# Uneven column pieces in three of the four key/value projection tiles of a decoder step

## The chip, the cores and the metric

The kernel runs on one core of one Trainium2 chip. The metric is device time in microseconds (us) of one execution; lower is better. TensorE is called PE here, its weight loads PEld, VectorE DVE, ScalarE ACT, GpSimd POOL and SyncE SP.

## What is computed

One inference step of a two-layer decoder over 1024 prompt tokens and 64 sample tokens (8 sequences of 8), 1088 token columns in all, with a model width of 2048. Layer 0 is a gated convolution mixer, layer 1 a sliding-window attention that reads one shared key/value projection. The part that matters here is that projection:

```python
kv = rms_norm(h, kv_norm) @ w_kv          # (tokens, 2048) @ (2048, 512)
k, v = jnp.split(kv, 2, axis=-1)          # 4 key/value heads of 64 each
```

Its inputs and outputs are float32. The result is needed for the attention of layer 1 and for the key and value caches that the step returns.

## The kernel before

All projections are made by one routine, `tile(n, z)` of the TensorE program (from line 499). A tile is one block of 128 output features for all 1088 token columns; there are 132 of them, each with 2048 input features in 16 steps `k` of 128. The activations lie in SBUF as `u_hi[128, 16, 1088]` and `u_lo[128, 16, 1088]`, and the weights of a tile as `w_hi` and `w_lo` in four quarters of 4 steps each: every float32 value is split into a rounded part (type float32r) and a rest. A product is the sum of three: hi by hi (line 512), hi weights by the rest of the activations (line 513), and the rest of the weights by hi (line 515).

One PSUM accumulator `z` has three banks of 512 float32 columns, `z[128, 3, 512]`. A matrix product writes one bank, so the 1088 columns go in three pieces, set by the table `CHUNKS`: columns 0 to 363, 364 to 727 and 728 to 1087. A step `k` thus issues nine matrix products: line 512 and line 513 for the first piece, the same for the second and the third, and then line 515 for the three pieces. Each product has a weight load of its own (128 rows by 128 columns) ahead of it in the trace. A tile makes 16 x 9 = 144 products.

```python
for c in cs:
    o = z[:, c, 0:CHUNKS[c][1]]
    pe.matmul(o, w_hi[:, q, at:at + P], chunk(u_hi[:, k, :], c), start=(i == 0), stop=False)
    pe.matmul(o, w_hi[:, q, at:at + P], chunk(u_lo[:, k, :], c), start=False, stop=False)
for c in cs:
    mm = pe.matmul(z[:, c, 0:CHUNKS[c][1]], w_lo[:, q, at:at + P], chunk(u_hi[:, k, :], c),
                   start=False, stop=(i == KT - 1))
```

The key/value projection is tiles 64 to 67 (`N_KV` is 64). Even tiles write `z_even`, odd ones `z_odd`. The two V tiles (64, 65) come first, then the two K tiles (66, 67). Their order on PE is written out by hand: tile 64, interleaved with the sums of squares of the residual stream (`sum_sq`, line 526); a wait for the root of the norm; tile 65; tile 66; then the transposes of V (lines 595 and 598), which use `aux`, and which wait for ACT's copies (lines 900 and 903); then tile 67. After that come the query and gate tiles (68 to 99), with the attention between their steps.

Three things surround a tile. SP loads its weights by quarters (`load_w`). For tiles 64 to 99 POOL multiplies a quarter by the norm's gain (`gain_w`, line 1005), ACT rounds it to `w_hi` once PE has used the same quarter of the tile before (`split_w`, line 730), and POOL subtracts to get `w_lo` (`rest_w`, line 1013); PE waits for that quarter by quarter. When PE has used all four quarters, DVE reads the accumulator by the same three pieces, multiplies it by the norm factor and writes it to SBUF (`read_z`, line 1261), and a later tile may use the accumulator again. After tile 67 ACT waits for that read, issues three DMAs for K (lines 914 to 916), and only then rounds the weights of tile 68.

Of the kernel before, what the change touches and what calls it, by code (L numbers as in the profile page):

```python
# [31 lines left out]
ALU = mybir.AluOpType  # L32
# [3 lines left out]
P = 128  # L36
D = 2048
KT = D // P
# [2 lines left out]
TS = SB * SS  # L41
T = TP + TS
CHUNKS = [(0, 364), (364, 364), (728, 360)]
ALL, HEAD, TAIL = (0, 1, 2), (0, 1), (2,)
TH = CHUNKS[2][0]
TT = T - TH
# [10 lines left out]
N_GLU, N_GATE, N_OUTA, N_KV, N_QG, N_OUTB, N_OUTC, N_END = 0, 32, 48, 64, 68, 100, 116, 132  # L57
# [32 lines left out]
def trunk_kernel(nc, x_t, state_t, ck_t, cv, w, cols_in, y_t, scp_t, ckp_t, cvp, scs_t, cks_t, cvs):  # L90
    ctx = ExitStack()
    with ctx:
        def sb(name, shape, dt=F32):
            return ctx.enter_context(nc.sbuf_tensor(name, shape, dt))
# [13 lines left out]
        u_hi = sb("u_hi", [P, KT, T], F32R)  # L108
        u_lo = sb("u_lo", [P, KT, T], F32R)
        w_raw = sb("w_raw", [P, NQ, 512])  # L110
        w_hi = sb("w_hi", [P, NQ, 512], F32R)
        w_lo = sb("w_lo", [P, NQ, 512], F32R)
# [8 lines left out]
        z_odd = ctx.enter_context(nc.psum_tensor("z_odd", [P, 3, 512], F32))  # L121
        z_even = ctx.enter_context(nc.psum_tensor("z_even", [P, 3, 512], F32))
        aux = ctx.enter_context(nc.psum_tensor("aux", [P, 2, 512], F32))
        ZS = [z_even, z_odd]
        aux1 = aux[:, :, :].rearrange("p a b -> p (a b)")

        def region(at, n):
            return work[:, at:at + n]
# [12 lines left out]
        cs = cs_flat.rearrange("p (b s) -> p b s", b=SB)  # L141
# [18 lines left out]
        r_b = region(0, T)  # L160
        kvb = [region(6 * T, T), region(7 * T, T), region(8 * T, T), region(9 * T, T)]
# [116 lines left out]
        def ge(eng, s, v):  # L278

            if not (isinstance(v, int) and v <= 0):  # L280
                eng.wait_ge(s, v)

        def chunk(ap, c):
            return ap[:, CHUNKS[c][0]:CHUNKS[c][0] + CHUNKS[c][1]]

# [210 lines left out]

        @block.tensor
        def _(pe):
            def tile(n, z, before_k=None, after_k=None, order=range(KT), cs=ALL):

                ge(pe, z_read, n - 1)
                seen = [0] * NQ
                for i, k in enumerate(order):
                    if before_k is not None:
                        before_k(i)
                    q, at = k // 4, P * (k % 4)
                    if seen[q] == 0:
                        pe.wait_ge(w_lo_ready, NQ * n + q + 1)
                    seen[q] += 1
                    for c in cs:  # L510
                        o = z[:, c, 0:CHUNKS[c][1]]
                        pe.matmul(o, w_hi[:, q, at:at + P], chunk(u_hi[:, k, :], c), start=(i == 0), stop=False)  # L512
                        pe.matmul(o, w_hi[:, q, at:at + P], chunk(u_lo[:, k, :], c), start=False, stop=False)  # L513
                    for c in cs:
                        mm = pe.matmul(z[:, c, 0:CHUNKS[c][1]], w_lo[:, q, at:at + P], chunk(u_hi[:, k, :], c),  # L515
                                       start=False, stop=(i == KT - 1))
                    if seen[q] == 4:
                        mm.then_inc(w_used, 1)
                    if after_k is not None:
                        after_k(i)  # L520

            def sum_sq(i):

                pe.wait_ge(sq_ready, KT + i + 1)
                for c in range(3):
                    mm = pe.matmul(z_odd[:, c, 0:CHUNKS[c][1]], ones[:, :], chunk(sq_h[i % 2], c),
                                   start=(i == 0), stop=(i == KT - 1))
                mm.then_inc(sq_summed, 1)

            def sum_o(phase):  # L530


                first, cs, _, added = PROJ[phase]
                pe.wait_ge(o_added, added + KT - 1)
                pe.wait_ge(z_read, first + KT - 1)
                for c in cs:
                    pe.matmul(z_even[:, c, 0:CHUNKS[c][1]], ones[:, :], chunk(acc_o, c), start=True, stop=False)
                pe.wait_ge(z_read, first + KT)
                for c in cs:
                    mm = pe.matmul(z_even[:, c, 0:CHUNKS[c][1]], ones[:, :], chunk(sq_o[1], c), start=False, stop=True)  # L540
                mm.then_inc(o_summed, 1)

            pe.wait_ge(consts_ready, 6)

            pe.transpose(aux[:, 0, 0:SS], causal_ts[0:SS, :], ident[0:SS, 0:SS]).then_inc(mask_turned, 1)
            tile(0, z_even, lambda k: pe.wait_ge(u_lo_ready, k + 1))
            pe.wait_ge(sq_added, KT - 1)
            for c in range(3):
                mm = pe.matmul(z_odd[:, c, 0:CHUNKS[c][1]], ones[:, :], chunk(r_a, c), start=True, stop=True)
            mm.then_inc(sq_summed, 1)  # L550
            pe.wait_ge(var_ready, 1)
            tile(1, z_odd)
            with pe.Fori(1, KT) as i:
                tile(2 * i, z_even)
                tile(2 * i + 1, z_odd)
# [27 lines left out]

            tile(N_KV, z_even, before_h, after_h, ORDER)
            pe.wait_ge(var_ready, 4)
            tile(N_KV + 1, z_odd)
            tile(N_KV + 2, z_even)

            for t in range(2):
                pe.wait_ge(z_read, N_KV + t + 1)  # L590
                for part in range(3):
                    ge(pe, vt_read, 3 * t + (1 if part == 2 else 0))
                    if part < 2:
                        for b in range(4):
                            mm = pe.transpose(aux[:, part, P * b:P * b + P],
                                              kvb[t][:, P * (4 * part + b):P * (4 * part + b) + P], ident[:, :])
                    else:
                        mm = pe.transpose(aux[0:TS, 0, 0:P], kvb[t][:, TP:T], ident[:, :])
                    mm.then_inc(vt_ready, 1)
            tile(N_KV + 3, z_odd)  # L600

            def scores(g, jj, u):

# [398 lines left out]
        def _(pool):  # L1002
# [143 lines left out]
            def add_o(j, par, phase):  # L1146
                first, cs, _, added = PROJ[phase]
                t0, t1 = CHUNKS[cs[0]][0], sum(CHUNKS[cs[-1]])
                pool.wait_ge(z_read, first + j + 1)
                ge(pool, o_added, added + j)  # L1150
                pool.tensor_tensor(acc_o[:, t0:t1], acc_o[:, t0:t1], sq_o[par][:, t0:t1], ALU.add
                                   ).then_inc(o_added, 1)
# [86 lines left out]
        def _(dve):  # L1239
# [14 lines left out]
                t0, t1 = CHUNKS[cs[0]][0], sum(CHUNKS[cs[-1]])  # L1254
                dve.reciprocal(r[:, t0:t1], r[:, t0:t1]).then_inc(r_ready, 1)

            def read_z(n, z, out, by):

                dve.wait_ge(w_used, NQ * (n + 1))
                for c in range(3):  # L1260
                    ins = dve.tensor_tensor(chunk(out, c), z[:, c, 0:CHUNKS[c][1]], chunk(by, c), ALU.mult)  # L1261
                ins.then_inc(z_read, 1)


# [17 lines left out]
            inv_rms(r_a, z_odd, 1)  # L1282
            dve.wait_ge(r_ready, 1)
            read_z(0, z_even, sig, r_a)

            def glu(j, nxt):
# [19 lines left out]
                for i in range(2, CW):  # L1306
                    if i > 2:
                        dve.wait_ge(tap, (CW - 1) * j + i - 2)
                    acc = odd_taps if i % 2 else aux1
                    dve.scalar_tensor_tensor(out=acc, in0=cp[:, i:i + TP],  # L1310
                                             scalar=cols[:, bass.ds(C_CW + j * CW + i, 1)], in1=acc,
                                             op0=ALU.mult, op1=ALU.add).then_inc(tap, 1)
                    if i == CW // 2 and nxt:
                        read_z(2 * j + 2, z_even, sig, r_a)
# [7 lines left out]


            read_z(N_GATE, z_even, gg0[0], r_a)
            dve.wait_ge(state_out, 32 * KT)
            for c in range(3):
# [8 lines left out]
                ins = dve.tensor_tensor(var, var, sq, ALU.subtract)  # L1335
# [54 lines left out]
            for i in range(1, 4):  # L1390
                dve.wait_ge(h_out[i], 16 * KT // 4)
            for t in range(4):
                read_z(N_KV + t, ZS[t % 2], kvb[t], r_b)

            def row_max(g, jj, u):

# [188 lines left out]
```

## Time and profile before

| | us |
|---|---|
| median of 3 runs | 3379.62 |
| lowest, highest run | 3376.69, 3385.57 |
| span of the profiled execution, first to last instruction | 3378.6 |
| PE busy, PEld busy (overlapping) | 3197.5, 3077.4 |
| DVE, ACT, POOL busy | 1511.2, 854.5, 1551.1 |
| mean granted clock of TensorE | 0.974 of full speed |

The profile gives no time of its own for that execution beside its span, which is 1.0 us below the median of the runs. Times in a row of a timeline are counted from the span's start. A matrix product's recorded length reaches past the start of the next one, because products are pipelined and their ends are modelled; the distance between starts tells what one costs in a stream. A weight load's recorded length likewise reaches past the start of the product that uses it.

### The profile page before, as it was taken

Reading aid. Unit: us, or ns where it says so; the run is one execution under the profiler, and the core shown is the slowest. Engines: PE = TensorE matmul, PEld = TensorE weight load, DVE = VectorE, ACT = ScalarE, POOL = GpSimd, SP = SyncE. Lnnn points to the kernel's source line nnn. Section 1 sums busy time; section 2 is a strip of 40 time slices with the busy share of each in tenths; the row PEclk is TensorE's granted clock in tenths of the full one; section 3 lists DMA queues with packets and bytes.
Section 4 is the critical chain, followed back from the end, with each engine's and each line's share of the span. In section 5 each row is a group of like instructions: output and inputs, shape, how many; then the busy total and the mean of one; then the engine's idle time right before and its main releaser. Section 6 shows DMA issues by size and latency. Waiting matters only on the chain.

```text
span 3378.6 us, 50475 instructions
## 1 busy us (share of the span) xinstructions
PE 3197.5 (95%) x19117; PEld 3077.4 (91%) x19117; DVE 1511.2 (45%) x1745; ACT 854.5 (25%) x1708; POOL 1551.1 (46%) x1153
## 2 busy tenths in 40 slices
PE   7999999999899999999778999999999999999995
PEld 6999999999899999999668998999899899899995
DVE  6999999999711131000560433244323343500043
ACT  5121121121222132212321322222222222332232
POOL 2777877878543324333353223332233223144475
PEclk9999999999899999999899999999999999899998
DMA  4122122122132252212453112111111211333386
GB/s 158 45 64 58 46 69 58 46 69 58 57 100 87 93 171 78 73 63 70 170 190 94 36 37 63 41 37 44 47 47 41 53 38 46 118 114 87 97 295 217
DMA packets 171677, 284.87 MB, mean 84 GB/s; under 512 B 62008, under 2 KB 72504, under 8 KB 171576
## 3 DMA queue, kind: packets, MB, share of 16 engines
q1 hardware_dynamic: 127328, 222.48, 22.2%
q10 hardware_dynamic: 41912, 52.32, 4.2%
q0 software_dynamic: 2352, 8.88, 0.7%
q8 instruction: 61, 1.00, 0.1%
q14 instruction: 24, 0.20, 0.0%
HBM read 218.44 MB, written 67.15 MB: 85 GB/s over the span
## 4 chain that ended last, share of the span: by engine, by line
PE 57%; POOL 17%; issue 12%; DVE 6%; DMA 4%; ACT 2%; SPq 1%; POOLq 0%; ACTq 0%; DVEq 0%
PE z_odd L512 9%; PE z_odd L513 8%; PE z_odd L515 8%; PE z_even L512 8%; PE z_even L513 7%; PE z_even L515 7%; POOL w_lo L1013 6%; POOL work L1094 4%; PE aux L609 3%; POOL work L1086 3%; PE z_even L627 2%; DMA work<-conv_scratch 1%; PE z_even L629 1%; POOL work L1122 1%; DMA work<-out_scratch 1%
## 5 line engine op out<-in xcount | busy, mean ns | idle before, releaser
L1013 POOL TENSOR_TENSOR w_lo<-w_raw,w_hi 128x512 fp32r<-128x512 f32 x528 | 746.7, 1423 | 1452.1 <-ACT w_hi L730 1451.6
L512 PE MATMUL z_even<-u_hi,w_hi 128*128 128x364 f32 (+1 forms) x2784 | 925.1, 332 | 80.7 <-POOL u_lo L1174 33.8
L512 PE MATMUL z_odd<-u_hi,w_hi 128*128 128x364 f32 (+1 forms) x2784 | 939.0, 337 | 58.9 <-POOL w_lo L1013 58.9
L513 PE MATMUL z_odd<-u_lo,w_hi 128*128 128x364 f32 (+1 forms) x2784 | 922.5, 331 | 0.0
L513 PE MATMUL z_even<-u_lo,w_hi 128*128 128x364 f32 (+1 forms) x2784 | 921.0, 331 | 0.0
L730 ACT ACTIVATE w_hi<-w_raw 128x512 fp32r<-128x512 f32 x528 | 331.4, 630 | 1730.5 <-PE z_even L515 810.3
L515 PE MATMUL z_odd<-u_hi,w_lo 128*128 128x364 f32 (+1 forms) x2784 | 636.5, 330 | 0.0
L515 PE MATMUL z_even<-u_hi,w_lo 128*128 128x364 f32 (+1 forms) x2784 | 635.3, 329 | 0.0
L512 PEld LDWEIGHTS z_even<-u_hi,w_hi 128*128 128x128 f32 x2784 | 529.8, 190 | 99.6 <-issue 30.7
L512 PEld LDWEIGHTS z_odd<-u_hi,w_hi 128*128 128x128 f32 x2784 | 531.7, 191 | 97.3 <-POOL w_lo L1013 55.1
L513 PEld LDWEIGHTS z_odd<-u_lo,w_hi 128*128 128x128 f32 x2784 | 532.1, 191 | 0.1
L513 PEld LDWEIGHTS z_even<-u_lo,w_hi 128*128 128x128 f32 x2784 | 530.2, 190 | 0.4 <-issue 0.3
L515 PEld LDWEIGHTS z_odd<-u_hi,w_lo 128*128 128x128 f32 x2784 | 487.9, 190 | 0.0
L515 PEld LDWEIGHTS z_even<-u_hi,w_lo 128*128 128x128 f32 x2784 | 486.6, 189 | 0.0
L1310 DVE SCALAR_TENSOR_TENSOR work<-work,cols 128x1024 f32<-128x1024 f32 x224 | 419.9, 1875 | 0.0
L1310 DVE SCALAR_TENSOR_TENSOR aux<-work,cols,aux 128x1024 f32<-128x1024 f32 x240 | 306.4, 1277 | 38.2 <-ACT aux L774 38.0
L1251 DVE TENSOR_SCALAR work<-z_even 128x364 f32<-128x364 f32 (+1 forms) x6 | 2.9, 529 | 657.0 <-PE z_even L540 657.0
L1261 DVE TENSOR_TENSOR work<-z_even,work 128x364 f32<-128x364 f32 (+1 forms) x126 | 59.4, 525 | 497.5 <-PE z_even L515 497.4
L1094 POOL TENSOR_TENSOR work<-work 128x480 f32<-128x480 f32 (+3 forms) x128 | 153.6, 1200 | 10.0
L1005 POOL TENSOR_TENSOR w_raw<-w_raw,cols 128x512 f32<-128x512 f32 x144 | 148.3, 1040 | 17.5 <-DMA branch_scratch<-work 17.5
L1086 POOL TENSOR_TENSOR work<-work,cols 128x248 f32<-128x248 f32 x128 | 130.4, 1049 | 2.9 <-POOL work L1098 2.9
L609 PE MATMUL aux<-work 64*128 64x256 f32 (+1 forms) x512 | 120.8, 376 | 0.0
(148 smaller groups left out, 2405.1 us busy)
## 6 DMA issues: line engine op xcount, KB each, us to landing
w_raw<-in_w SPq DMA_DIRECT2D x528, 256.0 KB, 2.7
work<-in_x SPq DMA_DIRECT2D x32, 544.0 KB, 5.7
work<-branch_scratch SPq DMA_DIRECT2D x31, 544.0 KB, 5.5
conv_scratch<-work ACTq DMA_DIRECT2D x16, 544.0 KB, 2.7
work<-conv_scratch SPq DMA_DIRECT2D x16, 544.0 KB, 3.7
resid_scratch<-work ACTq DMA_DIRECT2D x16, 544.0 KB, 6.2
branch_scratch<-work ACTq DMA_DIRECT2D x16, 512.0 KB, 2.6
branch_scratch<-work POOLq DMA_DIRECT2D x15, 544.0 KB, 3.0
```

What stands on the lines that cost most here:

```text
L512: pe.matmul(o, w_hi[:, q, at:at + P], chunk(u_hi[:, k, :], c), start=(i == 0), stop=False)
L513: pe.matmul(o, w_hi[:, q, at:at + P], chunk(u_lo[:, k, :], c), start=False, stop=False)
L515: mm = pe.matmul(z[:, c, 0:CHUNKS[c][1]], w_lo[:, q, at:at + P], chunk(u_hi[:, k, :], c), start=False, stop=(i == KT - 1))
L609: mm = pe.matmul(s_qk[:, i, lo:2 * BLK], qf[HD * p:HD * p + HD, BLK * b:BLK * b + BLK], kd[HD * p:HD * p + HD, BLK * (b - 1) + lo:BLK * b ...
L627: mm = pe.matmul(o, vd[:, b, :], pc[:, i, :], start=True, stop=(b == 0))
L730: act.activation(w_hi[:, q, :], w_raw[:, q, :], ACT.Copy).then_inc(w_hi_ready, 1)
L1005: pool.tensor_tensor(w_raw[:, q, :].rearrange("p (k c) -> p k c", k=4), w_raw[:, q, :].rearrange("p (k c) -> p k c", k=4), cols[:, gain + ...
L1013: pool.tensor_tensor(w_lo[:, q, :], w_raw[:, q, :], w_hi[:, q, :].bitcast(F32), ALU.subtract).then_inc(w_lo_ready, 1)
L1086: ins = pool.tensor_tensor(pr[:, b], win, cols[:, bass.ds(C_CW + j * CW, CW)].unsqueeze(1).to_broadcast([P, SS, CW]), ALU.mult)
L1094: pool.tensor_tensor(pm[:, :, 0:m], pm[:, :, 0:m], pm[:, :, other:other + m], ALU.add).then_inc(pool_step, 1)
L1261: ins = dve.tensor_tensor(chunk(out, c), z[:, c, 0:CHUNKS[c][1]], chunk(by, c), ALU.mult)
L1310: dve.scalar_tensor_tensor(out=acc, in0=cp[:, i:i + TP], scalar=cols[:, bass.ds(C_CW + j * CW + i, 1)], in1=acc, op0=ALU.mult, op1=ALU.add ...
```

## The change

Tile 64 keeps the pieces 364 + 364 + 360. Tile 65 takes 512 + 512 + 64 columns, tile 66 takes 512 + 448 + 128 and tile 67 takes 512 + 320 + 256. The number of products per tile, their order, their weights and the total of columns stay as they are. DVE's reads of the three accumulators are cut at the same places.

```diff
+KV_CUTS = [CHUNKS, [(0, 512), (512, 512), (1024, 64)], [(0, 512), (512, 448), (960, 128)],
+           [(0, 512), (512, 320), (832, 256)]]
...
-            def tile(n, z, before_k=None, after_k=None, order=range(KT), cs=ALL):
+            def tile(n, z, before_k=None, after_k=None, order=range(KT), cs=ALL, cuts=CHUNKS):
...
                     for c in cs:
-                        o = z[:, c, 0:CHUNKS[c][1]]
-                        pe.matmul(o, w_hi[:, q, at:at + P], chunk(u_hi[:, k, :], c), start=(i == 0), stop=False)
-                        pe.matmul(o, w_hi[:, q, at:at + P], chunk(u_lo[:, k, :], c), start=False, stop=False)
+                        t0, m = cuts[c]
+                        pe.matmul(z[:, c, 0:m], w_hi[:, q, at:at + P], u_hi[:, k, t0:t0 + m], start=(i == 0), stop=False)
+                        pe.matmul(z[:, c, 0:m], w_hi[:, q, at:at + P], u_lo[:, k, t0:t0 + m], start=False, stop=False)
                     for c in cs:
-                        mm = pe.matmul(z[:, c, 0:CHUNKS[c][1]], w_lo[:, q, at:at + P], chunk(u_hi[:, k, :], c),
+                        t0, m = cuts[c]
+                        mm = pe.matmul(z[:, c, 0:m], w_lo[:, q, at:at + P], u_hi[:, k, t0:t0 + m],
                                        start=False, stop=(i == KT - 1))
...
-            tile(N_KV + 1, z_odd)
-            tile(N_KV + 2, z_even)
+            tile(N_KV + 1, z_odd, cuts=KV_CUTS[1])
+            tile(N_KV + 2, z_even, cuts=KV_CUTS[2])
...
-            tile(N_KV + 3, z_odd)
+            tile(N_KV + 3, z_odd, cuts=KV_CUTS[3])
...
-            def read_z(n, z, out, by):
+            def read_z(n, z, out, by, cuts=CHUNKS):
 
                 dve.wait_ge(w_used, NQ * (n + 1))
-                for c in range(3):
-                    ins = dve.tensor_tensor(chunk(out, c), z[:, c, 0:CHUNKS[c][1]], chunk(by, c), ALU.mult)
+                for c, (t0, m) in enumerate(cuts):
+                    ins = dve.tensor_tensor(out[:, t0:t0 + m], z[:, c, 0:m], by[:, t0:t0 + m], ALU.mult)
...
-                read_z(N_KV + t, ZS[t % 2], kvb[t], r_b)
+                read_z(N_KV + t, ZS[t % 2], kvb[t], r_b, KV_CUTS[t])
```

## Rows read from the trace of the kernel before

**Rows 1.** The page: span, engines' busy time, and the chain's shares by engine.
```profile
span 3378.6 us, 50475 instructions
...
PE 3197.5 (95%) x19117; PEld 3077.4 (91%) x19117; DVE 1511.2 (45%) x1745; ACT 854.5 (25%) x1708; POOL 1551.1 (46%) x1153
...
PE 57%; POOL 17%; issue 12%; DVE 6%; DMA 4%; ACT 2%; SPq 1%; POOLq 0%; ACTq 0%; DVEq 0%
```
**Rows 2.** Waits of PE from 1735 to 1900 us: total us, times, longest.
```profile
PE z_even L512 <- POOL w_lo L1013: 5.4, 1, 5.4
PE z_odd L512 <- POOL w_lo L1013: 4.7, 1, 4.7
PE aux L598 <- ACT work L900: 3.1, 2, 2.7
```
**Rows 3.** Stretches of tiles 65, 66, 67: length, engines' busy us (count), granted clock, DMA share, GB/s.
```profile
1742.10:1768.30 26.20, 26.13 (x146) 26.16 (x147) 6.48 (x5) 3.16 (x5) 13.50 (x12) 0.91 0.26 71
1768.30:1791.90 23.60, 23.60 (x145) 23.58 (x144) 1.41 (x3) 2.53 (x4) 9.15 (x8) 1.00 0.41 128
...
1797.90:1823.40 25.50, 25.50 (x145) 25.29 (x145) 0.00 (x0) 0.62 (x2) 0.00 (x0) 0.93 0.19 54
```
**Rows 4.** Timeline of PE, tile 66 and its follower: start us, us, instruction [idle before].
```profile
1768.09 0.33 PE L512 MATMUL z_even<-u_hi,w_hi 128*128 128x364 f32 x1
...
1790.39 0.33 PE L512 MATMUL z_even<-u_hi,w_hi 128*128 128x364 f32 x1
...
1791.38 0.65 PE L515 MATMUL z_even<-u_hi,w_lo 128*128 128x364 f32 x3
1791.88 1.03 PE L595 MATMUL aux<-ident,work 128*128 128x128 f32 x8
```
**Rows 5.** Timeline of the weight loads, end of tile 66.
```profile
1790.39 0.19 PEld L513 LDWEIGHTS z_even<-u_lo,w_hi 128*128 128x128 f32 x1
1790.56 0.19 PEld L512 LDWEIGHTS z_even<-u_hi,w_hi 128*128 128x128 f32 x1
```
**Rows 6.** Timeline of the weight loads, a restart within tile 64.
```profile
1699.85 0.19 PEld L512 LDWEIGHTS z_even<-u_hi,w_hi 128*128 128x128 f32 x1 [1.86 <-POOL u_lo L1174]
1699.96 0.19 PEld L513 LDWEIGHTS z_even<-u_lo,w_hi 128*128 128x128 f32 x1
```
**Rows 7.** Timeline of PE, the same restart.
```profile
1699.86 0.43 PE L512 MATMUL z_even<-u_hi,w_hi 128*128 128x364 f32 x1 [1.28 <-POOL u_lo L1174]
1700.13 0.33 PE L513 MATMUL z_even<-u_lo,w_hi 128*128 128x364 f32 x1
```
**Rows 8.** Timeline of the weight loads, start of tile 65.
```profile
1742.14 0.29 PEld L512 LDWEIGHTS z_odd<-u_hi,w_hi 128*128 128x128 f32 x1 [5.22 <-issue]
1742.31 0.33 PEld L513 LDWEIGHTS z_odd<-u_lo,w_hi 128*128 128x128 f32 x1
```
**Rows 9.** Timeline of PE, first steps of tile 65.
```profile
1742.61 0.51 PE L513 MATMUL z_odd<-u_lo,w_hi 128*128 128x364 f32 x1
...
1745.03 0.51 PE L512 MATMUL z_odd<-u_hi,w_hi 128*128 128x364 f32 x1
```
**Rows 10.** Timeline of PE: the last sum of squares, six float32 products.
```profile
1735.50 1.99 PE L526 MATMUL z_odd<-work,ones 128*128 128x364 f32 x6
```
**Rows 11.** Line 526: ns min/median/max, first and last start us, forms.
```profile
L526 PEld LDWEIGHTS z_odd<-work,ones x96: 187/189/331, 1663.7 to 1736.7; 128*128 128x128 f32 x96
L526 PE MATMUL z_odd<-work,ones x96: 466/467/808, 1664.0 to 1737.0; 128*128 128x364 f32 x64, 128*128 128x360 f32 x32
```
**Rows 12.** Timeline of DVE: the read of tile 65.
```profile
1768.29 1.42 DVE L1261 TENSOR_TENSOR work<-z_odd,work 128x364 f32<-128x364 f32 x3 [19.69 <-PE z_odd L515]
```
**Rows 13.** The chain of waits between tiles 67 and 68: start us, us, what.
```profile
1823.53 1.43 DVE work L1261 x3
...
1828.85 0.67 PE z_even L512
```
**Rows 14.** Timeline of POOL: the last quarter of tile 66's weights.
```profile
1769.06 1.29 POOL L1013 TENSOR_TENSOR w_lo<-w_raw,w_hi 128x512 fp32r<-128x512 f32 x1 [4.66 <-ACT w_hi L730]
```

## The prediction, made before the changed kernel was run

> **What bounds the kernel now.** I read the page first, then the waits of PE around the changed tiles, then busy time by stretch, and last the timelines at single products, where the prices are. On the page PE is busy 95% of the span and holds 57% of the chain that ended last [rows 1]. That is an average, so the next view asks about the place itself. From 1735 to 1900 us PE waits only between tiles: 4.7 us ahead of tile 65, 3.1 us at the transposes behind tile 66, 5.4 us ahead of tile 68 [rows 2]. Inside tiles 65, 66 and 67 it never waits; in the stretch of tile 66 it is busy 23.60 of 23.60 us at a granted clock of 1.00, and the other engines are below half [rows 3]. So these tiles last as long as their 144 products do.
>
> The waits between tiles all end with work that itself follows PE. Behind tile 67 the chain goes from DVE's read through ACT and POOL to the first product of tile 68, 5.3 us after the read began [rows 13]. Nothing independent of PE is waited for there, so a microsecond more inside a tile is a microsecond at the end of the kernel. In turn nothing gets late: the last quarter of tile 66's weights is ready at 1770.35 [rows 14], and PE needs it three quarters into the tile, at 1768.09 + 0.75 x 23.79 = 1785.9 us.
>
> **What a product costs.** Tile 66 runs from 1768.09 to the first transpose at 1791.88: 23.79 us, 165.2 ns a product. Fifteen steps from 1768.09 to 1790.39 give 1.487 us a step, which is the same [rows 4]. What does that consist of? At the start of tile 65, at the lower level of the clock (1.2 GHz), eight products of 5 x 364 + 3 x 360 = 2900 columns take 1745.03 - 1742.61 = 2.42 us [rows 9]: one column per cycle, and nothing on top. At 2.4 GHz a step's 3 x 1088 = 3264 columns are 1360 ns, so 127 ns are left over, **14.1 ns a product**. I take this as a fixed price per product and the columns as proportional.
>
> The second resource is the weight load. Each product has its own, and it starts when the product ahead of it starts: both have 1790.39 [rows 4, 5]. So it has to fit behind one product. Its recorded length is 0.19 us, longer than the 0.17 us to the next one [rows 5], so the length cannot be the pace. The pace shows where PE restarts from idle at the full clock: the first load begins at 1699.85 and the second at 1699.96 [rows 6], while the first product needs until 1700.13 [rows 7]. The second load could begin because the first was done and its product had started. A load of 128 columns thus takes **0.11 us**; the 0.17 us from the second load to the second product's row are then a normal product. I use 109 ns (the starts before rounding). A piece of m columns then costs the larger of 109 ns and 14.1 + m/2.4 ns.
>
> **The change, part by part.** The number of products and of loads stays, and the columns stay. Only a piece whose own time is below 109 ns loses: the next load is then late.
>
> - 512 columns: 227.4 ns; 448: 200.8; 320: 147.4; 256: 120.8. All cover the load.
> - 128 columns: 67.4 ns, so 109 is paid, 41.6 lost. 64 columns: 40.8 ns, 68.2 lost.
> - Each piece stands three times in a step, 48 times in a tile. Tile 65: 48 x 68.2 = 3.27 us. Tile 66: 48 x 41.6 = 2.00 us. Tile 67: 0.
> - At the lower clock, in the first 4.6 us of tile 65, the load takes at most 0.17 us (1742.14 to 1742.31, [rows 8]), and 64 columns take 53 ns: 117 ns lost instead of 68. Some 1.5 steps of three pieces lie there, about 0.2 us more. Tile 67 also starts at that level, but 256 columns are 213 ns there and cover 170.
> - DVE's reads stay three instructions over 1088 columns, 1.42 us. For tiles 65 and 66 they run beside PE, after 19.69 us of idle time [rows 12]. For tile 67 the read is on the path [rows 13], but its sum stays, and it starts only when the whole tile is done. I take zero, within 0.1 us. Were that cover gone in the earlier tiles, 1.4 us each would be the price.
>
> The sum is 3.27 + 2.00 + 0.2 = **+5.5 us**. The profiled span of 3378.6 becomes 3384.1; it lies 1.0 us below the median of the runs, so I forecast 3379.6 + 5.5 = **3385.1 us**, or 0.16%.
>
> **Bounds.** No row shows a float32r product with few columns. The 14.1 ns can be of two kinds. In the sums of squares six float32 products span 1.99 us, and a product is recorded at 467 ns, so their distance is (1.99 - 0.47)/5 = 304 ns [rows 10, 11]; 364 columns at two cycles each are 303.3. There almost nothing is added, although the weight load is as long, 189 ns [rows 11]. If the 14.1 ns are the late end of a load, a long piece would not pay them. With 2.5 ns a product in their place the three tiles change by +2.2, +0.9 and -1.7 us: +1.4 us in all, the low end. The high end is that the same 165.2 ns are the least that any pair of load and product costs; this is the first rival. I stay with the fixed price because a load measured alone takes 109 ns, far below 165.
>
> **The rivals.**
>
> *The load's pace is 165 ns, not 109 (slower).* Then the distance of 165.2 ns is the weight load, and every piece of up to some 390 columns costs that. A 512 piece would cost 216. Tile 65: 48 x (216 + 216 + 165.2) = 28.67 us against 23.79, +4.9; tile 66: 48 x (216 + 189 + 165.2) = 27.37, +3.6; tile 67: 48 x (216 + 2 x 165.2) = 26.23, +2.4. In all +10.9 us, 3390.5. It decides the sign from a pace of about 150 ns on. For it speaks that PEld is busy 91% [rows 1], and that the columns do not account for the whole 165. Against it speak the two loads 0.11 us apart [rows 6], that a load is recorded just as long behind products 304 ns apart [rows 11], and that at the lower clock the columns alone account for the time [rows 9].
>
> *Nothing but columns counts (no change).* If loads ran further ahead than one product, short pieces would be filled by long ones: three pieces a step, the same columns, 0 us, 3379.6. Against it: every load in a dense stream begins with the product ahead of it and not earlier [rows 4, 5]. The Trainium skill, "TensorE: Matmul & The Clock Gate", section "Back-to-back issue gap", gives N/2.4 + 2.5 ns for an isolated product, by which this rival would come out; that page of the skill adds that it leaves out the weight load at small N, and here it gives 154 where the rows have 165.2. The same page of the Trainium skill, section "The mechanism" (in its part on packing), says that a load overlaps running products only in another row group. By that rule each pair would be serial, and uneven pieces would cost nothing either; the trace disagrees, since 109 + 152 = 261 ns would then be the distance, not 165.2.
>
> *The fixed price falls away for long pieces* (the low end above): +1.4 us, 3381.0.
>
> *Short products stream more slowly.* A float32 product takes two cycles a column, and line 526 leaves two records per product, so four cycles in all [rows 10, 11]. If a short float32r piece fell back to that, 64 columns would cost 107 + 14 = 121 ns and 128 columns 227: 12 and 118 ns above my price, 48 times each, 6.2 us more, 3391.3. Nothing in the trace suggests it. If 256 columns did so too, 15 us more would come on top, a case I leave outside.
>
> **How the numbers follow.** Chances: forecast 0.60, load pace of 165 ns 0.17, columns alone 0.10, vanishing fixed price 0.08, slow short products 0.05. The runs before lie 8.9 us apart, and each restart of PE at the lower clock may cost 1 or 2 us more or less when the work shifts, so a median can move by some 2 us either way. The cases reach from 3379.6 to 3391.3; I give 3378 to 3392. A measurement here tells about 0.3% from no change, 10.1 us. Faster by that much needs something that no case has: 0.02. Slower needs +10.1: the slow rivals sit at +10.9 and +11.7, so some two thirds of their 0.22, and a little of the forecast's own spread: 0.20. Within 0.3%: 0.78.
>
> **What would show it right or wrong.** In the changed trace, tile 65 should last some 3.4 us longer, tile 66 25.8 us and tile 67 as before. Two products of 64 or 128 columns in a row should start about 109 ns apart, two of 512 about 227. If the short ones are 165 apart, and pieces of 256 too, the first rival holds; 216 for a piece of 512 speaks for the vanishing price; 40 to 70 for the short ones means that loads run ahead. A new wait of PE inside a tile, or a stretch of tile 66 at a lower granted clock, would mean that something I left out decides.

## The result, and the profile after

The changed kernel took 3390.60 us (median of 5 runs, 3386.51 to 3400.17) beside 3381.58 us of the kernel before (5 runs, 3376.69 to 3385.84): a ratio of 1.0029, with a 95% interval of 1.0015 to 1.0042. It is slower, by about as much as a measurement here can tell; the time lies inside the forecast range, 5.5 us above the forecast itself. The profiled execution took 3392.1 us, with a span of 3390.5. The page's first lines stand beside [rows 1]:

```profile
span 3390.5 us, 50475 instructions
...
PE 3210.3 (95%) x19117; PEld 3079.9 (91%) x19117; DVE 1510.9 (45%) x1745; ACT 854.8 (25%) x1708; POOL 1551.7 (46%) x1153
```

PE's records, 19117 of each kind, are as many as before, and PE is busy 12.8 us longer. The waits of PE in the stretch from 1735 to 1912 us answer to [rows 2] (who waited for whom: us in total, times, longest; the tile routine's lines are two or three higher in the changed file):

```profile
PE z_even L514 <- POOL w_lo L1016: 5.4, 1, 5.4
PE z_odd L514 <- POOL w_lo L1016: 4.7, 1, 4.7
PE aux L601 <- ACT work L903: 3.1, 2, 2.7
```

The three waits between the tiles are the same to a tenth. Nothing was turned into a new wait, so the time lies inside the tiles. The stretches of tiles 65, 66 and 67 (length, busy us and count of PE, PEld, DVE, ACT and POOL, granted clock, DMA share, GB/s), beside [rows 3]:

```profile
1744.60:1774.50 29.90, 29.83 (x145) 25.22 (x145) 6.46 (x4) 3.15 (x5) 13.47 (x12) 0.92 0.21 62
1774.50:1800.80 26.30, 26.30 (x147) 23.42 (x146) 1.42 (x3) 2.53 (x4) 9.12 (x8) 1.00 0.38 115
1806.70:1832.40 25.70, 25.65 (x145) 23.18 (x145) 0.00 (x0) 0.65 (x2) 0.00 (x0) 0.93 0.20 56
```

PE is still busy without a gap, at granted clocks within 0.01 of those before. New is PEld: where it filled the stretches before, it now has gaps, since loads wait behind the long pieces. Two bounds of tiles in the kernel before, the first products of tiles 65 and 67, stand beside [rows 4, 13]:

```profile
1742.17 0.65 PE L512 MATMUL z_odd<-u_hi,w_hi 128*128 128x364 f32 x1 [4.68 <-POOL w_lo L1013]
...
1797.92 0.65 PE L512 MATMUL z_odd<-u_hi,w_hi 128*128 128x364 f32 x1
```

After the change the timeline of PE has the tiles' bounds, the start of tile 65's second step, and one of its steps at the full clock; the last line is DVE's read of tile 67 (start us, us, instruction, idle before it and what ended that):

```profile
1744.67 0.77 PE L514 MATMUL z_odd<-u_hi,w_hi 128*128 128x512 f32 x1 [4.68 <-POOL w_lo L1016]
...
1747.86 0.78 PE L514 MATMUL z_odd<-u_hi,w_hi 128*128 128x512 f32 x1
...
1757.27 0.48 PE L514 MATMUL z_odd<-u_hi,w_hi 128*128 128x512 f32 x1
1757.58 0.39 PE L515 MATMUL z_odd<-u_lo,w_hi 128*128 128x512 f32 x1
1757.81 0.40 PE L514 MATMUL z_odd<-u_hi,w_hi 128*128 128x512 f32 x1
1758.05 0.39 PE L515 MATMUL z_odd<-u_lo,w_hi 128*128 128x512 f32 x1
1758.28 0.19 PE L514 MATMUL z_odd<-u_hi,w_hi 128*128 128x64 f32 x1
1758.31 0.27 PE L515 MATMUL z_odd<-u_lo,w_hi 128*128 128x64 f32 x1
1758.41 0.74 PE L518 MATMUL z_odd<-u_hi,w_lo 128*128 128x512 f32 x3
1758.99 0.48 PE L514 MATMUL z_odd<-u_hi,w_hi 128*128 128x512 f32 x1
...
1774.47 0.48 PE L514 MATMUL z_even<-u_hi,w_hi 128*128 128x512 f32 x1
...
1800.77 1.04 PE L598 MATMUL aux<-ident,work 128*128 128x128 f32 x8
...
1806.85 0.47 PE L514 MATMUL z_odd<-u_hi,w_hi 128*128 128x512 f32 x1
...
1815.17 0.28 PE L514 MATMUL z_odd<-u_hi,w_hi 128*128 128x256 f32 x1
1815.29 0.28 PE L515 MATMUL z_odd<-u_lo,w_hi 128*128 128x256 f32 x1
...
1832.50 1.42 DVE L1264 TENSOR_TENSOR work<-z_odd,work 128x512 f32<-128x512 f32 x3 [30.11 <-PE z_odd L518]
```

| | before, us | after, us | gained |
|---|---|---|---|
| tile 65, first product to that of tile 66 | 25.92 | 29.80 | 3.88 |
| tile 66, first product to the first transpose | 23.79 | 26.30 | 2.51 |
| tile 67, first product to DVE's read | 25.61 | 25.65 | 0.04 |

A step of tile 65 lasts 1758.99 - 1757.27 = 1.72 us, where it was 1.487. The starts of short products mislead: the second product of 64 columns is recorded 0.03 us after the first, and the next long one 0.10 us later, as if there were no floor. A product's recorded start does not tell when its weights were there. The loads do:

```profile
1757.24 0.19 PEld L514 LDWEIGHTS z_odd<-u_hi,w_hi 128*128 128x128 f32 x1
1757.35 0.19 PEld L515 LDWEIGHTS z_odd<-u_lo,w_hi 128*128 128x128 f32 x1
1757.58 0.19 PEld L514 LDWEIGHTS z_odd<-u_hi,w_hi 128*128 128x128 f32 x1
1757.81 0.19 PEld L515 LDWEIGHTS z_odd<-u_lo,w_hi 128*128 128x128 f32 x1
...
1758.28 0.19 PEld L515 LDWEIGHTS z_odd<-u_lo,w_hi 128*128 128x128 f32 x1
1758.39 0.54 PEld L518 LDWEIGHTS z_odd<-u_hi,w_lo 128*128 128x128 f32 x3
1758.96 0.19 PEld L514 LDWEIGHTS z_odd<-u_hi,w_hi 128*128 128x128 f32 x1
1759.07 0.19 PEld L515 LDWEIGHTS z_odd<-u_lo,w_hi 128*128 128x128 f32 x1
```

Loads stand 0.11 us apart where a piece of 64 columns runs beside them (1757.24 to 1757.35, 1758.28 to 1758.39), and 0.23 us where one of 512 does. Three times 109 ns leave (1720 - 327)/6 = 232.2 ns of the step for each of the six long pieces.

The tiles gained 6.4 us, and the two spans differ by 11.9. Of the rest, 2.5 us lie ahead of the first changed instruction (1742.17 became 1744.67), where the two programs are alike, and 3.0 behind tile 67. The mean granted clock was 0.972 instead of 0.974 of full speed: some 190 us of this span at the lower level instead of 178. These 12 us more, at half the speed, can hold 6 us, about what is left to explain; that is an estimate. Whether the change has a part in that rest was the first question for the experiments.

### The profile page after: what moved, and what is told of

Same layout as the page of the kernel before. It is cut to its first block, busy times and chain, and to the rows that moved or that the text cites. A ratio compares the mean times of both kernels' runs of the same rounds, so it can differ in the third digit from the quotient of the medians.

```text
span 3390.5 us, 50475 instructions
## 1 busy us (share of the span) xinstructions
PE 3210.3 (95%) x19117; PEld 3079.9 (91%) x19117; DVE 1510.9 (45%) x1745; ACT 854.8 (25%) x1708; POOL 1551.7 (46%) x1153
## 4 chain that ended last, share of the span: by engine, by line
PE 57%; POOL 17%; issue 12%; DVE 6%; DMA 4%; ACT 2%; SPq 0%; POOLq 0%; ACTq 0%; DVEq 0%
PE z_odd L514 9%; PE z_odd L515 8%; PE z_odd L518 8%; PE z_even L514 7%; PE z_even L515 7%; PE z_even L518 7%; POOL w_lo L1016 7%; POOL work L1097 4%; PE aux L612 3%; POOL work L1089 3%; PE z_even L630 2%; DMA work<-conv_scratch 1%; PE z_even L632 1%; DMA work<-out_scratch 1%; POOL work L1125 1%
## 5 line engine op out<-in xcount | busy, mean ns | idle before, releaser
L514 PE MATMUL z_even<-u_hi,w_hi 128*128 128x364 f32 (+3 forms) x2784 | 925.5, 332 | 83.6 <-POOL u_lo L1177 33.6
L514 PE MATMUL z_odd<-u_hi,w_hi 128*128 128x364 f32 (+3 forms) x2784 | 942.7, 339 | 55.0 <-POOL w_lo L1016 55.0
L515 PE MATMUL z_odd<-u_lo,w_hi 128*128 128x364 f32 (+3 forms) x2784 | 923.8, 333 | 0.0
L515 PE MATMUL z_even<-u_lo,w_hi 128*128 128x364 f32 (+3 forms) x2784 | 919.8, 331 | 0.0
L518 PE MATMUL z_odd<-u_hi,w_lo 128*128 128x364 f32 (+3 forms) x2784 | 641.5, 332 | 0.0
L518 PE MATMUL z_even<-u_hi,w_lo 128*128 128x364 f32 (+3 forms) x2784 | 635.1, 329 | 0.0
L1264 DVE TENSOR_TENSOR work<-z_even,work 128x364 f32<-128x364 f32 (+2 forms) x126 | 59.5, 526 | 501.1 <-PE z_even L518 501.0
L612 PE MATMUL aux<-work 64*128 64x256 f32 (+1 forms) x512 | 120.8, 376 | 0.0
```

Source lines behind the costliest of these rows:

```text
L514: pe.matmul(z[:, c, 0:m], w_hi[:, q, at:at + P], u_hi[:, k, t0:t0 + m], start=(i == 0), stop=False)
L515: pe.matmul(z[:, c, 0:m], w_hi[:, q, at:at + P], u_lo[:, k, t0:t0 + m], start=False, stop=False)
L518: mm = pe.matmul(z[:, c, 0:m], w_lo[:, q, at:at + P], u_hi[:, k, t0:t0 + m], start=False, stop=(i == KT - 1))
L612: mm = pe.matmul(s_qk[:, i, lo:2 * BLK], qf[HD * p:HD * p + HD, BLK * b:BLK * b + BLK], kd[HD * p:HD * p + HD, BLK * (b - 1) + lo:BLK * b ...
L1264: ins = dve.tensor_tensor(out[:, t0:t0 + m], z[:, c, 0:m], by[:, t0:t0 + m], ALU.mult)
```

## The experiments

Two questions were open. Does the change cost more than its tiles? And what are the prices: a fixed one per product with a floor of 109 ns, as predicted, or another?

**The kernel before, beside itself** (no edit).

> The unchanged kernel beside itself, for the size of what moves without any edit. Theory (the 6.4 us that the three tiles gained are the change's whole effect, and the rest of the 11.9 us between the two profiled spans is where TensorE's lower clock level fell): a ratio of 1.000 with an interval of about 0.15% either way, tiles 65, 66 and 67 at 26.1, 23.8 and 25.6 us as before, and a total time at the lower level that differs from the 178 us of the first profile by several us. Rival (the excess is a further effect of the change): the time at the lower level is 178 us again, within 2 us, and the span 3378.6 within 1 us.

Measured: 3382.15 us beside 3382.51, ratio 1.0003 (0.9994 to 1.0011). The profile is no help to either side: its span is 3378.6 us again, with a time at the lower level of 181 us. The runs tell more: 12 of the same program lie between 3377.81 and 3384.99 us. A difference of 3 us between two single profiles is within that.

**Tile 65 alone**

```diff
-KV_CUTS = [CHUNKS, [(0, 512), (512, 512), (1024, 64)], [(0, 512), (512, 448), (960, 128)],
-           [(0, 512), (512, 320), (832, 256)]]
+KV_CUTS = [CHUNKS, [(0, 512), (512, 512), (1024, 64)], CHUNKS, CHUNKS]
```

> Only tile 65 in pieces of 512 + 512 + 64, all others as before. Theory: tile 65 lasts 30.0 us instead of 26.1, tiles 66 and 67 stay at 23.8 and 25.6, and the whole is 3.9 us longer, a ratio of 1.001. Rival (a further effect follows each uneven tile, as the whole change cost more than its tiles): 5 us or more longer, a ratio of 1.0015 to 1.002.

Measured: 3383.40 us beside 3382.51, ratio 1.0009 (1.0000 to 1.0018). From the first product of tile 65 to that of tile 66 the profile has 29.69 us, and the two other tiles are as before within 0.1 us. The ratio fits 1.0012, the tile's own gain of 3.9 us; it does not quite exclude the lower part of the rival's range.

**All three tiles long**

```diff
+KV_CUTS = [CHUNKS] + 3 * [[(0, 512), (512, 320), (832, 256)]]
```

> Tiles 65, 66 and 67 all in pieces of 512 + 320 + 256, none short. Theory (a piece loses only where its columns take less than the 109 ns of the next weight load): 256 columns take 117 ns, so nothing changes, tiles 26.1, 23.8 and 25.6 us, ratio 1.000. Rival of the prediction (a weight load's pace is 165 ns): 2.4 us more in each tile, 7.3 us in all, ratio 1.002.

Measured: 3379.92 us beside 3382.51, ratio 0.9998 (0.9989 to 1.0007). Tile 66 in the timeline of PE, from its first product to the first transpose:

```profile
1770.58 0.40 PE L513 MATMUL z_even<-u_hi,w_hi 128*128 128x512 f32 x1
...
1794.42 0.38 PE L597 MATMUL aux<-ident,work 128*128 128x128 f32 x2
```

That is 23.84 us instead of 23.79. Three pieces as uneven as 512, 320 and 256 cost nothing. A load with a pace of 165 ns would have shown 2.4 us a tile; that rival falls.

**Half as wide weights**

```diff
-                        pe.matmul(z[:, c, 0:m], w_hi[:, q, at:at + P], u_hi[:, k, t0:t0 + m], start=(i == 0), stop=False)
+                        pe.matmul(z[0:wc, c, 0:m], w_hi[:, q, at:at + wc], u_hi[:, k, t0:t0 + m], start=(i == 0), stop=False)
...
-            tile(N_KV + 1, z_odd, cuts=KV_CUTS[1])
+            tile(N_KV + 1, z_odd, cuts=KV_CUTS[1], wc=64)
```

The other products of the three tiles and DVE's reads are narrowed alike.

> The change, with only the first 64 of the 128 output features computed in tiles 65, 66 and 67, so that each weight load has 64 columns instead of 128; the other 64 features of K and V are left out, and so their result is not that of the reference. Theory (the floor of a short piece is the weight load, about 55 ns for 64 columns): two pieces of 64 columns stand 55 ns apart instead of 109, pieces of 128 columns 58 ns instead of 110; tile 65 is back to about 27 us and tile 66 to 23.8. Rival (a short product has a floor of its own): 109 ns stays, tile 65 at 30.0 and tile 66 at 26.3 us. It also tells where the price beyond 1/2.4 ns a column comes from: if the weight load that runs beside a product slows it, a piece of 512 falls from 232 to about 223 ns; if the stream itself is slower, it stays at 232.

The weight loads of one step of tile 65:

```profile
1756.65 0.13 PEld L514 LDWEIGHTS z_odd<-u_hi,w_hi 128*64 128x64 f32 x1
1756.71 0.14 PEld L515 LDWEIGHTS z_odd<-u_lo,w_hi 128*64 128x64 f32 x1
1756.94 0.13 PEld L514 LDWEIGHTS z_odd<-u_hi,w_hi 128*64 128x64 f32 x1
...
1757.63 0.13 PEld L515 LDWEIGHTS z_odd<-u_lo,w_hi 128*64 128x64 f32 x1
1757.69 0.43 PEld L518 LDWEIGHTS z_odd<-u_hi,w_lo 128*64 128x64 f32 x3
1758.21 0.13 PEld L514 LDWEIGHTS z_odd<-u_hi,w_hi 128*64 128x64 f32 x1
```

Beside a piece of 64 columns the loads are now 55 ns apart (1756.65 to 1756.71, 1757.63 to 1757.69 before rounding), half of 109. The step is 1.56 us, and tile 65 lasts 26.95 us. So **the floor of a short piece is the weight load**. These products also have half as many outputs; that this is not the reason shows in the two-byte run below, where 64 columns with all 128 outputs take 28 ns. The long pieces did not move: (1560 - 3 x 55.5)/6 = 232 ns for 512 columns. What they cost beyond 1/2.4 ns a column is not the load that runs beside them. Tile 66 came out shorter than expected, 23.52 us instead of 23.8: its step is 1467 ns where 0.4545 ns a column gives 3 x 1088 x 0.4545 = 1484. So prices of single pieces are good to a few ns, no better, and the cause of that difference is open.

**Pieces just under 256 columns**

```diff
+KV_CUTS = [CHUNKS, [(0, 448), (448, 448), (896, 192)], [(0, 480), (480, 384), (864, 224)],
+           [(0, 512), (512, 336), (848, 240)]]
```

> Pieces just under 256 columns: tile 65 in 448 + 448 + 192, tile 66 in 480 + 384 + 224, tile 67 in 512 + 336 + 240. Read is the length of one of the 16 steps of a tile at the full clock, 1487 ns before. Theory (0.4545 ns a column, no fixed price, and at least 109 ns a piece): 1549, 1505 and 1483 ns. The prediction's law (14.1 ns a product and 1/2.4 ns a column, at least 109 ns): 1532, 1492 and 1487 ns. Rival (pieces of fewer than 256 columns stream at the price of float32, four cycles a column): 192 columns 320 ns, steps over 2000 ns in all three tiles.

Measured: steps of 1547, 1507 and 1493 ns in tiles 65, 66 and 67 (1549, 1505 and 1483 by the price per column, 1532, 1492 and 1487 by the prediction's law). The loads of a step in tile 65:

```profile
1751.80 0.19 PEld L514 LDWEIGHTS z_odd<-u_hi,w_hi 128*128 128x128 f32 x1
1751.91 0.19 PEld L515 LDWEIGHTS z_odd<-u_lo,w_hi 128*128 128x128 f32 x1
1752.11 0.19 PEld L514 LDWEIGHTS z_odd<-u_hi,w_hi 128*128 128x128 f32 x1
...
1753.35 0.19 PEld L514 LDWEIGHTS z_odd<-u_hi,w_hi 128*128 128x128 f32 x1
```

192 columns still pay the load's 0.11 us, and a piece of 448 takes 0.20 to 0.21 us. In the two tiles where the laws are far apart, the price per column is right within 2 ns a step. At 240 columns, which should just cover the load, the step is 10 ns above it and 6 above the prediction's law: at the edge neither is exact. The rival of a float32 price for pieces under 256 columns is gone by more than 400 ns a step.

**Two-byte operands**

```diff
+                    def weights(w):
+                        return w[:, q, at:at + P // 2].bitcast(F16) if half else w[:, q, at:at + P]
+
+                    def moving(u):
+                        return u[:, k, t0:t0 + m // 2].bitcast(F16) if half else u[:, k, t0:t0 + m]
```

> The change, with weights and activations of tiles 65, 66 and 67 read as two-byte float16 values, as many columns as before from half the bytes; the numbers of K and V are then meaningless. It asks what the 0.4545 ns a column are, which at 2.4 GHz should be 0.4167. Theory (the reading of four-byte columns from SBUF limits the stream): a piece of 512 falls from 232 to about 216 ns, 448 to 189, 320 to 136. Rival (it is the stream itself or the writing of PSUM): 232, 204 and 146 ns stay. In both cases the weight load is shorter or equal, so pieces of 128 columns take 54 to 58 ns instead of 109 if two-byte loads take half as long.

One step of tile 65 in the timeline of PE:

```profile
1756.24 0.38 PE L521 MATMUL z_odd<-u_hi,w_hi 128*128 128x512 f16 x1
1756.46 0.38 PE L522 MATMUL z_odd<-u_lo,w_hi 128*128 128x512 f16 x1
...
1757.10 0.19 PE L521 MATMUL z_odd<-u_hi,w_hi 128*128 128x64 f16 x1
1757.13 0.19 PE L522 MATMUL z_odd<-u_lo,w_hi 128*128 128x64 f16 x1
1757.16 0.63 PE L525 MATMUL z_odd<-u_hi,w_lo 128*128 128x512 f16 x3
1757.62 0.38 PE L521 MATMUL z_odd<-u_hi,w_hi 128*128 128x512 f16 x1
```

The step is 1.38 us, and it is the same in all three tiles: 512 columns take 216 ns, 64 columns 28 to 29. That is 1/2.4 ns a column and 2.5 ns a product, and the short pieces cost no more than their columns because two-byte loads are so much shorter: a load starts beside the piece of 64 columns at 1757.10, and the next load follows it after 28 ns (before rounding), at 1757.13.

```profile
1757.11 0.10 PEld L522 LDWEIGHTS z_odd<-u_lo,w_hi 128*128 128x128 f16 x1
```

So the higher price of a column belongs to four-byte operands, as the theory had it. Whether it is the reading from SBUF or the way the array takes such a value in, this run does not tell, since both changed.

**The cost 32 times over**

```diff
-                tile(n, z_even)
+                tile(n, z_even, cuts=QCUT)
...
-                tile(n + 1, z_odd, None, beside)
+                tile(n + 1, z_odd, None, beside, cuts=QCUT)
```

Here `QCUT` is 512 + 512 + 64; DVE's reads of these tiles are cut alike, and the key/value tiles are as before.

> The suspected cost 32 times over: the 32 query and gate tiles (68 to 99) in pieces of 512 + 512 + 64, the key/value tiles as before. Theory: a step grows from 1487 to 1720 ns, a tile by 3.73 us, 119 us in all, and all of it reaches the end since PE hardly waits there: about 3501 us, ratio 1.035. Rival (a part is taken up by waits of PE for the attention's other engines between the steps): less than 100 us, ratio under 1.030. Second rival (each uneven tile costs the whole more than its own length): more than 140 us.

Measured: 3494.47 us beside 3382.83, which is 111.6 us, ratio 1.0333 (1.0317 to 1.0348). Neither expectation held: it lies between the theory's 119 and the rival's 100. DVE's reads of tiles 68, 69 and 70 tell which tiles fall short, first in the kernel before, then here:

```profile
1854.38 1.42 DVE L1261 TENSOR_TENSOR work<-z_even,work 128x364 f32<-128x364 f32 x3 [29.43 <-PE z_even L515]
...
1895.91 1.42 DVE L1261 TENSOR_TENSOR work<-z_odd,work 128x364 f32<-128x364 f32 x3 [0.99 <-PE z_odd L515]
1919.70 1.42 DVE L1261 TENSOR_TENSOR work<-z_even,work 128x364 f32<-128x364 f32 x3 [22.37 <-PE z_even L515]
```

```profile
1860.05 1.42 DVE L1264 TENSOR_TENSOR work<-z_even,work 128x512 f32<-128x512 f32 x3 [33.22 <-PE z_even L518]
...
1904.76 1.42 DVE L1264 TENSOR_TENSOR work<-z_odd,work 128x512 f32<-128x512 f32 x3 [1.17 <-PE z_odd L518]
1932.28 1.42 DVE L1264 TENSOR_TENSOR work<-z_even,work 128x512 f32<-128x512 f32 x3 [26.10 <-PE z_even L518]
```

The plain tile 70 went from 23.79 to 27.52 us, by 3.73 as expected. Tile 69, which has the attention's products between its steps, went from 41.53 to 44.71, by 3.18 only. Over 16 pairs of tiles that is 16 x (3.73 + 3.18) = 110.6 us. PE does not wait longer inside that tile. Rather, in 9 of its 16 steps the last short piece is followed by a product of the attention instead of the tile's next step, and the weight loads tell what becomes of the piece's loss there:

```profile
1863.38 0.41 PEld L612 LDWEIGHTS aux<-work 64*128 64x128 f32 x3 [0.15 <-issue]
```

In five of the nine places (four times scores, as here, and once values) the attention's first load does not run beside the short piece at all. It begins 0.12 us after that piece (1863.26 to 1863.38); in the kernel before it began 0.26 us after a piece of 360 columns at the same place (1856.98 to 1857.24), and the 0.14 us between the two are the 296 columns. So there is nothing that a short piece could make late. In the other four places transposes follow. Their load does run beside the short piece, but it takes 0.06 us instead of 0.11 (1877.59 to 1877.64, 59 ns before rounding), so 0.03 us is lost instead of 0.08, and the four groups of transposes are 0.03 us longer each. Five losses of 0.08 us and four of 0.045 us that are missing make 0.57 us, where 3.73 - 3.18 = 0.55 was missing. This is read from the starts in the two traces; no run of its own isolates it.

**The same tiles, long** (`QCUT` is 512 + 320 + 256).

> The same 32 tiles in pieces of 512 + 320 + 256. Theory: 1490 ns a step, as in the run with three such tiles, which is 0.05 us a tile and under 2 us in all, ratio 1.000. Rival of the prediction (a weight load's pace is 165 ns): 2.4 us a tile, 78 us in all, ratio 1.023. If it comes out faster by more than 0.1%, such pieces would be the better cut for the kernel.

Measured: 3382.78 us beside 3382.83, ratio 1.0000 (0.9991 to 1.0009). A plain tile takes 23.84 us. Within the 3 us of the interval nothing is lost in 32 tiles, and nothing won.

**The change again, and three tiles short.** The first is the changed kernel without an edit, the second has

```diff
+KV_CUTS = [CHUNKS] + 3 * [[(0, 512), (512, 512), (1024, 64)]]
```

> The change itself once more, in more runs. Theory (the tiles' own 6.4 us are all that it costs, and the 9 us between the first medians are chance): a ratio of 1.0019, with 1.0 to 1.003 as the interval, and tiles 65, 66 and 67 at 30.0, 26.3 and 25.6 us again. Rival (a further effect of 2 to 4 us on top): a ratio of 1.0025 to 1.003, whose interval leaves 1.0019 out.

> Tiles 65, 66 and 67 all in pieces of 512 + 512 + 64. Theory: 1720 ns a step in each, 3.73 us a tile and 0.2 us more where the clock is at its lower level, 11.4 us in all, a ratio of 1.0034. Rival (a further effect of the change beyond its tiles): 15 us or more, ratio 1.0045.

| run | expected of the tiles' own, us | as a ratio | measured ratio, 95% interval |
|---|---|---|---|
| tile 65 alone | 3.9 | 1.0012 | 1.0009 (1.0000 to 1.0018) |
| the change again | 6.4 | 1.0019 | 1.0019 (1.0010 to 1.0028) |
| three tiles short | 11.4 | 1.0034 | 1.0033 (1.0021 to 1.0046) |

In the change again the tiles lasted 29.59, 26.30 and 25.65 us, the first some 0.2 us shorter than in the first profile. With three short tiles the step at the full clock is 1720 ns in each, but the tiles lasted 29.60, 27.52 and 30.57 us: the last is 5.0 us longer than in the kernel before, not 3.9. Around the start of tile 67 the clock was at its lower level (granted clock 0.50) from 1807.36 to 1814.20 there, twice as long as in the kernel before (1797.91 to 1801.31). So the three tiles gained 12.4 us in that profile, a ratio of 1.0037, still within the interval. No interval is narrow enough to exclude 2 us more by itself, but all three middles stand within 0.0003 of what was expected of the tiles. By the repeat the change costs 6.4 us, between 3.4 and 9.5; that the first five runs showed 9 is within their own interval, 5 to 14 us, and needs no cause.

No cut with all of K and V computed beats the kernel before: those with all pieces of 256 columns or more are equal to it, the others have longer steps.

## Why the prediction was right, and where its size was off

*What bounds the stretch.* Right. PE is busy throughout in the changed tiles, the waits between them kept their lengths, and the microseconds in the tiles came out at the end: 111.6 us in the run with 32 short tiles, where the growth of tiles 69 and 70, 16 times over, is 110.6.

*The load takes 109 ns and is the floor.* Right. Read from two loads at a restart [rows 6, 7], it came back as the distance of loads beside pieces of 64 columns, and it halved with half as wide weights. The Trainium skill, "TensorE: Matmul & The Clock Gate", section "LDWEIGHTS (loading the stationary operand)", gives columns/1.2 ns, by estimate 107 for 128 columns; 109 and 55 ns for 128 and 64 four-byte columns agree with it, the 28 ns of a load of 128 two-byte columns do not.

*The price of a piece, 14.1 ns fixed and 1/2.4 ns a column.* This is the step that was mis-sized. In one size of piece, 360 or 364 columns, a fixed and a proportional price look the same; I chose the fixed one, and the runs showed the other: 232 ns for 512 columns instead of 227.4, 117 instead of 120.8 for 256. With 0.4545 ns a column and no fixed part, 64 columns are 29 ns, not 40.8, so a short piece loses 80 ns and the long ones pay for all their columns. Two groups of rows that were at hand spoke against a fixed price: at 1.2 columns a nanosecond, at the lower clock [rows 9] and in the float32 sums [rows 10, 11], there was next to nothing on top. A small fixed part is not excluded: 232.2 ns for 512 columns and 165.2 for 363 on average give 0.449 ns a column and 2.5 ns a product as well, which differs from 0.4545 by less than 4 ns a step in every tile here.

| | forecast, us | measured, us |
|---|---|---|
| tile 65, 16 steps at the full clock | +3.27 | 16 x (1720 - 1487) ns = +3.73 |
| tile 66 | +2.00 | +2.51 |
| tile 67 | 0 | +0.04 |
| lower clock, rest of tile 65 | +0.2 | 3.88 - 3.73 = +0.15; in the repeat 3.67 - 3.73 = -0.06 |
| sum | +5.5 | +6.4; in the repeat +6.2 |

The +0.15 does not bear the forecast's +0.2 out. From tile 65's first product on, the clock stayed at its lower level (granted clock 0.50) for 4.53 us in the kernel before, for 4.93 us in the first profile after the change and for 4.49 us in the repeat; 0.4 us more at half the speed are 0.2 us by themselves. The first step, all of it at that level, grew by 0.33 us (from 1745.03 - 1742.17 to 1747.86 - 1744.67), 0.10 more than at the full clock, where the forecast had 3 x (117 - 68) = 0.15. But longer steps also mean that fewer of the 16 fall into the stretch at the lower level. With stretches of nearly equal length, 4.53 and 4.49 us, the two cancel: 3.67 us beside 3.73.

The median of the first runs, 9.0 us above that of the kernel before, is above both sums. It lies 5.5 us above the forecast time: 2.0 of them because the kernel before had 3381.58 us in these runs instead of 3379.62, 0.9 by the mis-sized price, and the last 2.6 did not come back in the repeat, so they count as chance. They took it to within 1.4 us of the end of the range. The repeat stands at 1.0019, close to the forecast's 1.0016.

*The bounds.* The low end had the extra price fall away for long pieces, and the runs went the other way: long pieces pay more of it. The high end, a pace of 165 ns, was excluded by the tiles of 512 + 320 + 256.

*The rivals.* Columns alone: excluded, a short piece costs its load. Slow short products: excluded, 192 columns cost 109 ns, and 64 columns 55 ns beside a load of half the width. The vanishing fixed price: excluded, 512 columns cost 19 ns more than 512/2.4, not 2.5. The formula of the Trainium skill that was weighed there, "TensorE: Matmul & The Clock Gate", section "Back-to-back issue gap", N/2.4 + 2.5 ns, fits two-byte operands within 1 ns, down to 28 to 29 ns for 64 columns, where the load is short; for float32r it is 16 ns too low at 512 columns.

*DVE's reads at nothing.* Right: 1.42 us for any cut, as [rows 12] had it.

## What to carry to other kernels

Where every product has its own weight load, a product costs the longer of its own columns and the load that runs beside it, which is the next product's. With four-byte operands at the full clock a piece needs some 240 columns to cover a load of 128 columns of weights, 109 / 0.4545; with all pieces at 256 columns or more it made no difference how uneven they were, and below some 240 each piece loses the difference. One size of piece cannot tell a fixed price from a proportional one: before extrapolating to another size, find a second size in the trace, or keep both laws as the bounds. A short stretch at the lower clock moved a single tile by more than 1 us from profile to profile, so prices are best read from steps at the full clock.

## What the runs showed of the hardware that was not expected

Float32r columns stream at 0.45 ns at the full clock, 8 to 9% above 1/2.4, and float16 columns at 1/2.4 ns with 2.5 ns a product. Half as long weight loads did not change it, and at the lower clock it is absent: 2900 columns took 2.42 us [rows 9]. It is absent in the float32 sums of squares too, 304 ns for 364 columns at two cycles each [rows 10, 11]. So it looks like a limit of some 2.2 four-byte columns a nanosecond, which neither of these two reaches with 1.2; what sets it stayed open.

A load of 128 two-byte columns does not hold back products 28 to 29 ns apart, so it takes about a fourth of the four-byte load's 109 ns, or less.

The recorded start of a product after a short piece is no sign that its weights are there: after a piece of 64 columns it came 0.08 us before its load could have ended. Lengths of steps and starts of loads are what can be trusted.
